# Sixteen of a convolution's 128 VectorE steps moved into the stage before, the rest spread evenly over eight heads

## The reference

```python
a, gt = jnp.split(conv_in, 2, axis=-1)
z = a * jax.nn.sigmoid(gt)
z = lax.conv_general_dilated(z, rhs, window_strides=(1,), padding=[(30, 0)],
    dimension_numbers=("NWC", "WIO", "NWC"), feature_group_count=512)   # 31 taps, per channel
z = layer_norm(z + conv_b, ln_g, ln_b)
conv_out = silu(z) @ w_conv_out
merged = gates[0] * conv_out + gates[1] * mla_out
```

## Time and profile before

| what | value |
|---|---|
| median of 3 runs | 1405.42 us (1405.08 to 1405.69) |
| the profiled execution | 1405.74 us |
| its span | 1403.9 us |
| TensorE, matmuls | 1382.0 us busy, 98% |
| TensorE, weight loads | 1111.6 us, 79% |
| VectorE | 783.9 us, 56% |
| ScalarE | 600.3 us, 43% |
| GpSimd | 73.7 us, 5% |
| DMA | 126.67 MB, mean 90 GB/s |

### The profile page before, as it was taken

How to read it: one execution, slowest core, us unless ns; L and a number is a source line. 1 busy time by engine, 2 the same in 40 slices (tenths; PEclk the granted TensorE clock), 3 DMA queues, 4 the chain that set the end, 5 groups by cost and what they waited for, 6 DMA issues and landing times.

```text
span 1403.9 us, 19004 instructions
## 1 busy us (share of the span) xinstructions
PE 1382.0 (98%) x6429; PEld 1111.6 (79%) x6429; DVE 783.9 (56%) x1248; ACT 600.3 (43%) x1012; POOL 73.7 (5%) x60
## 2 busy tenths in 40 slices
PE   7999999989999999999999999999999999999998
PEld 6787777768878888888888888778778778778886
DVE  7438888865466544345545486465465465455553
ACT  6535655555455442214333385344344344343233
POOL 1000000101103000000023300000000000000000
PEclk9999999999999999999999999999999999999999
DMA  5323323223322333324333323323323322323332
GB/s 157 90 71 78 73 56 98 75 93 104 119 85 81 99 96 104 105 60 118 91 90 106 103 75 95 94 64 89 93 65 88 93 68 85 93 71 95 105 105 76
DMA packets 228143, 126.67 MB, mean 90 GB/s; under 512 B 17107, under 2 KB 220964, under 8 KB 228099
## 3 DMA queue, kind: packets, MB, share of 16 engines
q1 hardware_dynamic: 226482, 123.47, 30.4%
q10 hardware_dynamic: 1616, 2.62, 0.5%
HBM read 123.98 MB, written 2.10 MB: 90 GB/s over the span
## 4 chain that ended last, share of the span: by engine, by line
PE 95%; ACT 2%; DVE 2%; issue 1%; DMA 0%; ACTq 0%; DVEq 0%
PE lin L609 26%; PE lin L613 26%; PE lin L612 26%; PE ob L724 2%; PE sc L688 1%; PE sc L711 1%; PE tr L700 1%; PE tr L1035 1%; PE tr L653 0%; PE tr L711 0%; PE ob L700 0%; DMA xtok<-in_x_dram 0%; PE sc L972 0%; PE sc L1091 0%; PE sc L1088 0%
## 5 line engine op out<-in xcount | busy, mean ns | idle before, releaser
L1570 DVE TENSOR_TENSOR wl<-raw,wh 128x1024 fp32r<-128x1024 f32 x238 | 287.4, 1214 | 184.4 <-ACT wh L1132 179.5
L1132 ACT ACTIVATE wh<-raw 128x1024 fp32r<-128x1024 f32 x238 | 239.2, 1012 | 117.7 <-DMA raw<-in_w_mlp_dram 44.8
L609 PE MATMUL lin<-uh,wh 128*128 128x512 f32 x624 | 252.0, 404 | 2.2 <-DVE gates L1825 1.0
L613 PE MATMUL lin<-uh,wl 128*128 128x512 f32 x624 | 243.4, 390 | 0.0
L612 PE MATMUL lin<-ul,wh 128*128 128x512 f32 x624 | 243.3, 390 | 0.0
L609 PE MATMUL lin<-vh,wh 128*128 128x512 f32 x576 | 232.2, 403 | 0.0
L613 PE MATMUL lin<-vh,wl 128*128 128x512 f32 x576 | 225.4, 391 | 0.0
L612 PE MATMUL lin<-vl,wh 128*128 128x512 f32 x576 | 224.3, 389 | 0.0
L609 PEld LDWEIGHTS lin<-uh,wh 128*128 128x128 f32 x624 | 117.2, 188 | 30.4 <-issue 4.1
L612 PEld LDWEIGHTS lin<-ul,wh 128*128 128x128 f32 x624 | 117.3, 188 | 25.0 <-issue 2.6
L613 PEld LDWEIGHTS lin<-uh,wl 128*128 128x128 f32 x624 | 117.1, 188 | 25.0
(11 more groups left out here) (478 smaller groups left out, 1889.8 us busy)
## 6 DMA issues: line engine op xcount, KB each, us to landing
raw<-in_w_in_dram SPq DMA_DIRECT2D x100, 512.0 KB, 3.8
raw<-in_w_mlp_dram SPq DMA_DIRECT2D x64, 512.0 KB, 4.0
raw<-in_w_out_dram SPq DMA_DIRECT2D x16, 512.0 KB, 3.5
raw<-in_w_xkv_dram SPq DMA_DIRECT2D x8, 512.0 KB, 3.6
raw<-in_w_proj_b_dram SPq DMA_DIRECT2D x8, 512.0 KB, 3.5
raw<-in_w_proj_a_dram SPq DMA_DIRECT2D x8, 512.0 KB, 3.6
xtok<-in_x_dram ACTq DMA_DIRECT2D x4, 512.0 KB, 5.3
raw<-in_w_mla_out_dram SPq DMA_DIRECT2D x4, 512.0 KB, 3.4
```

The source lines that it names most:

```text
L609: ins = pe.matmul(o, wh[:, slot, at], xh_, start=start, stop=False)
L613: return pe.matmul(o, wl[:, slot, at], xh_, start=False, stop=stop)
L1132: act.activation(wh[:, c.slot(4), 0:size], raw[:, c.slot(2), 0:size], ACT.Copy).then_inc(hi_made, 1)
L1570: dve.tensor_tensor(wl[:, c.slot(4), 0:size], raw[:, c.slot(2), 0:size], wh[:, c.slot(4), 0:size].bitcast(F32), ALU.subtract).then_inc(lo_ ...
```

## The change

The 128 convolution steps get one running number, 32 x t + w. Sixteen of them, all of tile 0, are issued in the loop of the stage "conv", by the table `CONV_TAPS`: none at m = 0 and 1, one at m = 2, and three at each m from 3 to 7, each time as the last thing of that m, so after `z[t]` is made. The other 112 are issued by the heads, 14 in each: 2, 2, 4 and 6 in its four runs. The hardware loop over pairs of heads on VectorE is gone and all eight heads are written out, so that step numbers, columns and semaphore values are constants. The programs of the other engines are unchanged.

```diff
--- before.py
+++ after.py
@@ -109,6 +109,8 @@
            ("k", 3))
 
 MEM_TURNS = {0: {2: 0, 4: 1, 6: 2}, 1: {1: 3, 4: 4, 7: 5}, 2: {2: 6, 5: 7}}
+CONV_TAPS = (0, 0, 1, 3, 3, 3, 3, 3)
+HEAD_TAPS = (2, 2, 4, 6)
 NCONST = 4 + 16
 SEL_MADE = 7
 ROUND = 1.5 * 2.0 ** 23
@@ -1708,6 +1710,31 @@
             norm_apply("q", "q_norm_g", lambda f: cq[:, f, :], cqh, cql)
             dve.wait_ge(trig_made, 1)
             freed(dve.tensor_tensor(logit[:, 0:S], read(j + 5)[:], trig[:], ALU.mult), j + 5)
+
+            def tap(t, w):
+
+                zt, at = z[:, t, w:w + S], (acc[:, t, :], te[:])[w % 2]
+                tap_ = taps[:, TAPS * t + w:TAPS * t + w + 1]
+                if w == 0:
+                    return dve.tensor_scalar(at, zt, tap_, col("conv_b", t), ALU.mult, ALU.add)
+                if w == 1:
+                    return dve.tensor_scalar(at, zt, tap_, None, ALU.mult)
+                return dve.scalar_tensor_tensor(at, zt, tap_, at, ALU.mult, ALU.add)
+
+            tapped = [0]
+
+            def some_taps(count):
+
+                for k in range(tapped[0], tapped[0] + count):
+                    t, w = divmod(k, TAPS + 1)
+                    if w == 0:
+                        dve.wait_ge(z_made, t + 1)
+                    if k:
+                        dve.wait_ge(tap_done, k - (1 < w < TAPS))
+                    ins = tap(t, w) if w < TAPS else dve.tensor_tensor(acc[:, t, :], acc[:, t, :], te[:], ALU.add)
+                    ins.then_inc(tap_done, 1)
+                tapped[0] += count
+
             c, j = phase("conv")
             lower(c + 2)
             dve.wait_ge(kr_ready, 1)
@@ -1726,6 +1753,7 @@
                     th = (logit[:, 512:1024], pt[:, 0:512])[t % 2]
                     zt = z[:, t, PAD:PAD + S]
                     dve.scalar_tensor_tensor(zt, th, 1.0, zt, ALU.add, ALU.mult).then_inc(z_made, 1)
+                some_taps(CONV_TAPS[m])
 
 
             dve.wait_ge(z_made, CT)
@@ -1746,35 +1774,12 @@
                 run(3)
                 lower(c + 6)
 
-            def two_heads(c, j, t, n):
-                def tap(w):
-
-
-                    zt, at = z[:, t, w % TAPS:w % TAPS + S], (acc[:, t, :], te[:])[w % 2]
-                    k = (TAPS + 1) * t + w
-                    tap_ = taps[:, bass.ds(TAPS * t + w % TAPS, 1)]
-                    if w:
-                        dve.wait_ge(tap_done, k - (1 < w < TAPS))
-                    if w == 0:
-                        ins = dve.tensor_scalar(at, zt, tap_, cols[:, bass.ds(COL["conv_b"] + t, 1)], ALU.mult, ALU.add)
-                    elif w == 1:
-                        ins = dve.tensor_scalar(at, zt, tap_, None, ALU.mult)
-                    elif w < TAPS:
-                        ins = dve.scalar_tensor_tensor(at, zt, tap_, at, ALU.mult, ALU.add)
-                    else:
-                        ins = dve.tensor_tensor(acc[:, t, :], acc[:, t, :], te[:], ALU.add)
-                    ins.then_inc(tap_done, 1)
-
-                for p, cuts in ((0, (0, 2, 4, 8, 16)), (1, (16, 18, 20, 24, TAPS + 1))):
-                    head(c + 4 * p, j + 4 * p, n + p, p, lambda k: [tap(w) for w in range(cuts[k], cuts[k + 1])])
-                low(ol[:, t, :], ob[:], oh[:, t, :], o_high, (Idx(t) if isinstance(t, int) else Idx(0, 1, t)).times(1, 1),
-                    o_low)
-
             lower(phase("heads")[0] + 2)
-            with dve.Fori(0, CT - 1) as i:
-                two_heads(*phase("heads", 8, 8, i), i, Idx(0, 2, i))
-            c, j = phase("heads")
-            two_heads(c + 8 * (CT - 1), j + 8 * (CT - 1), CT - 1, Idx(2 * (CT - 1)))
+            for n in range(HEADS):
+                c, j = phase("heads")
+                head(c + 4 * n, j + 4 * n, Idx(n), n % 2, lambda k: some_taps(HEAD_TAPS[k]))
+                if n % 2:
+                    low(ol[:, n // 2, :], ob[:], oh[:, n // 2, :], o_high, n // 2 + 1, o_low)
 
 
             c, j = phase("mla_out")
```

## The result

The changed kernel takes 1408.09 us, the median of 22 runs (1406.99 to 1409.40), against 1405.74 us for the kernel before, also of 22 (1405.08 to 1406.61): a ratio of 1.0014, 95% interval 1.0009 to 1.0020. That is 2.35 us more, clear of zero, and still less than the 0.2% set as the bound of "no change".

The account below looks back on a forecast made before the run. TensorE was taken as the bound, VectorE mattering only where a step comes late for it. The terms 0 + 0 + 1.64 + 0 gave +1.6 us on 1405.42, so 1407.0 us, range 1405.3 to 1408.8 us.

Parts of the forecast that it names:

- What it adds at m = 7: Entry of the heads: three taps ahead of the lowering and `qt` delay TensorE by 1.64 us.
- What the change takes away: Heads: two taps fewer each, 10.6 us less VectorE work over eight; gain between 0 and 0.7 us, taken as 0.
- m = 2 to 6: Stage "conv": thirteen added taps, at most 8.6 us, covered by VectorE's idle time; cost 0.
- the writing-out: VectorE's heads: a longer instruction stream from writing out the loop, cost taken as 0.
- Rival A: Behind the pause at the heads' entry TensorE's clock falls, 1.5 us more, 3.1 us in all, 1408.5 us; 9 in 100.
- the pause is half as long as the one that did it: Argument against rival A: new pause about 2.1 us, against the 4.25 us wait followed by the lower clock.
- These move by the same 1.64 us: Head entry: q loads and ScalarE's `wh`, queued behind the three taps, move as the scores do and add nothing.
- rival B: VectorE's written-out heads wait for instruction loads: +2.5 to +3.4 us, some 1408.3 us; 8 in 100.
- rival C: Stall at the heads' entry hidden or absent: 0 to +0.8 us, 1405.8 us; 11 in 100.
- rival D: Less VectorE work in the heads speeds TensorE: 1404.7 us if only idle goes, 1402 otherwise; 4 in 100 each.
- the norm's piece of TensorE at 275.44 us: After the heads: TensorE's sending of the norm, on which the 5.3 us of waits in "conv_out" were said to hang.

Follow-up runs that it names:

- early splitting: Kernel before, with ScalarE's splitting of two weight chunks in "conv_out" moved ahead of the squares and the scaling of the memory rows: 1399.26 against 1405.60 us.
- the taps behind `qt`: Changed kernel with the three taps of m = 7 issued in head 0 behind `qt`, ahead of the next lowering: 1406.21 against 1405.60 us for the kernel before.
- the written-out kernel: Changed kernel with the old schedule, no tap in "conv" and 2, 2, 4, 8 in every written-out head: 1405.56 against 1405.72 us for the kernel before.

## Why the prediction was right

**The terms.** "What it adds at m = 7" was 1.64 us, measured 1.63 in the profile, and by the dose 0.30, 0.96, 1.63 and 3.61 us for one, two, three and six taps, where 0.665 each less 0.36 gives 0.30, 0.97, 1.64 and 3.63. "What the change takes away" was taken as 0, and is: TensorE's 39.52 of 39.70 us a pair didn't move. m = 2 to 6 and the writing-out were 0 and are. The lower cluster, 1407.12 us, lies 0.1 us from the 1407.0 forecast, which is closer than it deserves: the forecast stood on a median of three runs, 1405.42 us; on the 1405.74 of 22 runs it would have been 1407.4.

**What was mis-sized.** Rival A, the low clock behind the longer pause, was given 9 in 100 and thought of as one outcome of two for the kernel. It is an outcome of each execution. It came in about half of them: 12 of 22 if the upper cluster is all its own, 9 if only those with a mean clock of 0.995 are. Its price, 1.5 us, was right (1.46 between the clusters, 1.62 in the profile). So the median lies above the forecast, at 1408.09, just inside the upper cluster, 1.1 us from the 1407.0 of the forecast and 0.4 from rival A's 1408.5. The time was within the range because the range took in A; the sum by itself gives only the lower cluster. Which of the two clusters the median fell into is chance, with ten executions against twelve. I had argued "the pause is half as long as the one that did it", which is no reason: the traces of before held a wait of 4.25 us with the low clock behind it and ones of 0.33 and 1.02 without, and nothing between.

**The queue behind the taps.** "These move by the same 1.64 us" was wrong of the loads. The last of the three q loads of head 1 is issued at 106.82 instead of 104.94, 1.9 us later of which 0.25 were there before. But ScalarE's `wh`, which waits for them, comes at 110.46 instead of 106.84, after 4.97 us of idle instead of 1.60. With no or one tap at m = 7 it comes at 106.86 and 107.09, with two at 109.99: from two taps on the loads take 1.2 to 1.7 us more to land. Why is open. In the changed kernel it cost nothing: behind the low clock every matmul of head 0 keeps its distance. With two taps and no low clock it is the likely source of the 0.3 us at the first turn, since this `wh` stands ahead of the exponentials in ScalarE's program and these of `vtok`; at two taps with early splitting, where it comes 0.3 us sooner against the kv matmuls, TensorE loses less than 0.1 us there. The other miss of this kind is that of the taps behind `qt`: there I counted the three taps and forgot the two of the first run, which also stand ahead of the row maxima.

**VectorE's busy time.** A pair of heads was to lose 3 us (4 x 0.74) and lost 1.8, and "conv" was to gain 11 us and gained 10.1. A tap's record is 0.74 us long but the next starts after 0.66, so four taps are 2.65 us of busy time and not 3.0, and the 16 in "conv" are shorter in the same way. Of the rest in the heads 0.8 us has a cause that nobody waits for; it is told below.

**Also held:** rival B (code) is refuted by the written-out kernel, rival C by the wait itself, rival D by TensorE's unchanged share. The waits in "conv_out" were to stay at 5.3 us and are 4.3: the second one, 1.0 us, is gone, because the low clock lasted longer there in this execution and TensorE came so much later that nothing was left to wait for. That is not the change's doing: the profiled execution of the written-out kernel, with the old schedule, shows the same 4.3 us in one piece. The common shift is 3.50 us at 288 us and 3.51 at 310 us, and 3.52 at 470 us, so that cost nothing. What the prediction gave as their source, the norm's piece of TensorE at 275.44 us, was wrong: with early splitting that piece keeps its place in TensorE's program, and 4.6 of the 5.3 us are gone.

## What to carry to other kernels

Work moved into a stage where an engine is two thirds idle is free only where its idle time lies ahead of what others wait for. Look at the last item that the engine does in the stage, and at which of the steps behind it frees a buffer: three taps in front of such a step cost 0.665 us each less the slack, and thirteen at places with cover, nothing. The three behind `qt` freed the buffer in time and then cost some 0.8 us by another way, so the search has to go on to the next step that somebody waits for. And before an engine's load is evened out, ask whether anyone waits for it: the wait list of the bound engine pointed at "conv_out", two steps further back stood ScalarE's order of work, and two splits moved there brought 6.3 us.

## What the runs showed of the hardware

**The clock after a short pause.** TensorE's granted clock fell to 1.2 GHz after waits of 1.95 us in all three profiled executions that have one (the changed kernel twice, three taps with early splitting once), and it cost some 1.6 us each time. All three belong to the slower ones of their kernel. By the times and the mean clocks it happens in about half of the executions (9 to 12 of 22, and 4 of 7). After 3.94 us (six taps) and 4.2 us ("conv_out", nine profiled executions) it fell every time. After 0.3 and 0.6 us the clock stayed at 1.00 in all eight profiled executions, and after 1.29 us in both; one more run of two taps may have had the low clock, by its mean. One program thus has two times 1.5 us apart, and 3 runs of it can give either.

**VectorE beside GpSimd.** The step that opens a tile, one input from SBUF and a bias (line 1719), follows the tile's last step directly in the even schedule, and so meets GpSimd's sum, which the same last step releases. The timeline of the changed kernel, VectorE and then GpSimd:

```profile
173.34 0.70 DVE L1734 TENSOR_TENSOR conv<-conv,te 128x512 f32<-128x512 f32 x1
174.14 1.35 DVE L1719 TENSOR_SCALAR conv<-conv,taps,cols 128x512 f32<-128x512 f32 x1
175.52 0.49 DVE L1721 TENSOR_SCALAR te<-conv,taps 128x512 f32<-128x512 f32 x1
...
174.11 1.09 POOL L569 TENSOR_TENSOR ta<-conv 128x512 f32<-128x512 f32 x1 [124.23 <-DVE conv L1734]
```

The same of the kernel before, GpSimd and then VectorE:

```profile
178.09 2.01 POOL L567 TENSOR_TENSOR ta<-conv 128x512 f32<-128x512 f32 x1 [128.46 <-DVE conv L1765]
...
184.11 0.54 DVE L1759 TENSOR_SCALAR conv<-conv,taps,cols  x1
```

Together, VectorE's step takes 1.35 instead of 0.54 us and GpSimd's 1.09 instead of 2.01. The Trainium skill (Advanced Engine Details and Errata, section VectorE Performance Modes) says that VectorE's second SBUF port is shared with GpSimd and that the two block each other where VectorE runs in a two-port mode. The trace agrees as to the direction, with 0.81 us lost; in which mode this step ran it doesn't say. That GpSimd is faster beside this step than beside steps with two inputs (2.00 us at 258.86, beside a lowering) is in the rows too. Here the loss was covered.
